# Attention units placed inside the query and output projections of a decoder step, with rotary halves in tiles of their own

## What is computed

```python
q = (_rms(x, ln) @ w_q).reshape(B, L, N_HEADS, HEAD_DIM)      # 16 heads of 64, 4 K/V heads
q = _rope(_rms(q, q_norm), pos)       # rotary: halves x1, x2 of 32 -> x1 cos - x2 sin, x2 cos + x1 sin
s = einsum('...qhgd,...khd->...hgqk', q, k) * HEAD_DIM ** -0.5  # window of 128 keys back
s = where(mask, s, NEG_INF); m = maximum(max(s), sink); p = exp(s - m)
o = einsum('...hgqk,...khd->...qhgd', p / (sum(p) + exp(sink - m)), v)
x = x + o.reshape(B, L, N_HEADS * HEAD_DIM) @ w_o
```

## Time and profile before

| | |
|---|---|
| median of 3 runs | 1662.77 us (1653.1 to 1663.02) |
| the profiled execution, its time | 1662.77 us |
| its span, first to last instruction | 1661.0 us |
| TensorE busy | 1611.2 us (97%), 11258 matmuls |
| DVE, ACT, POOL busy | 818.8, 492.5, 153.5 us |
| mean granted TensorE clock | 0.975 |

### The profile page before, as it was taken

The page is one execution under the profiler, slowest core; times in us unless marked ns, Lnnn a source line. Parts: engine busy times, 40 slices in busy tenths (PEclk is TensorE's granted clock), DMA queues, the critical chain, the costliest instruction groups (busy, mean ns, idle before and its releaser), DMA issues.

```text
span 1661.0 us, 26879 instructions
## 1 busy us (share of the span) xinstructions
PE 1611.2 (97%) x11258; PEld 1466.0 (88%) x11258; DVE 818.8 (49%) x1018; ACT 492.5 (30%) x745; POOL 153.5 (9%) x147
## 2 busy tenths in 40 slices
PE   7999999999999899999999999989999999999997
PEld 7679868968967899999999998865599999999997
DVE  6447337527535754334434575456755443433342
ACT  4233143133223322222212351135723221222221
POOL 0010000001001420000000131222331000000001
PEclk9999999999999999999999999975999999999999
DMA  6346226217224152222232222100023222232223
GB/s 231 106 165 214 83 96 225 86 58 262 81 74 155 52 179 76 92 86 93 84 102 76 89 89 77 54 6 1 1 77 97 81 89 89 81 97 89 89 76 105
DMA packets 49678, 164.40 MB, mean 99 GB/s; under 512 B 5664, under 2 KB 5728, under 8 KB 49568
## 3 DMA queue, kind: packets, MB, share of 16 engines
q1 hardware_dynamic: 41472, 134.23, 24.7%
q0 software_dynamic: 7408, 26.78, 4.4%
q10 hardware_dynamic: 720, 2.26, 0.3%
HBM read 141.82 MB, written 23.46 MB: 100 GB/s over the span
## 4 chain that ended last, share of the span: by engine, by line
PE 90%; DVE 5%; DMA 2%; ACT 1%; issue 1%; POOL 0%; ACTq 0%; DVEq 0%; POOLq 0%
PE ps L354 67%; PE ps L368 8%; PE ps L841 2%; PE ps L1123 2%; PE ps L835 2%; PE ps L1145 2%; DVE arena L1165 1%; DMA out_st_s<-arena 1%; PE ps L823 1%; PE ps L1134 1%; PE ps L855 1%; DMA arena<-in_state 1%; DVE xg_lo L1171 1%; PE ps L1037 1%; DMA w_raw<-in_w 1%
## 5 line engine op out<-in xcount | busy, mean ns | idle before, releaser
L354 PE MATMUL ps<-xg_hi,w_hi 128*128 128x272 f32 x1728 | 360.5, 290 | 15.3 <-DVE xg_lo L1171 8.3
L354 PE MATMUL ps<-xg_hi,w_lo 128*128 128x272 f32 x1728 | 358.0, 289 | 0.0
L354 PE MATMUL ps<-xg_lo,w_hi 128*128 128x272 f32 x1728 | 356.8, 288 | 0.0
L337 ACT ACTIVATE w_hi<-w_raw 128x1024 fp32r<-128x1024 f32 x220 | 227.2, 1052 | 368.6 <-PE ps L354 209.5
L342 DVE TENSOR_TENSOR w_lo<-w_raw,w_hi 128x1024 fp32r<-128x1024 f32 x220 | 281.6, 1297 | 63.5 <-ACT w_hi L337 57.9
L354 PE MATMUL ps<-pr_hi,w_hi 128*128 128x272 f32 x1440 | 304.5, 291 | 7.0 <-DVE pr_lo L1165 3.7
L354 PE MATMUL ps<-pr_hi,w_lo 128*128 128x272 f32 x1440 | 301.3, 289 | 0.0
L354 PE MATMUL ps<-pr_lo,w_hi 128*128 128x272 f32 x1440 | 300.4, 288 | 0.0
L354 PEld LDWEIGHTS ps<-xg_hi,w_hi 128*128 128x128 f32 x1728 | 273.0, 189 | 25.7 <-issue 12.7
L354 PEld LDWEIGHTS ps<-xg_lo,w_hi 128*128 128x128 f32 x1728 | 272.1, 189 | 0.0
L354 PEld LDWEIGHTS ps<-xg_hi,w_lo 128*128 128x128 f32 x1728 | 270.3, 189 | 0.0
(11 more groups left out here) (198 smaller groups left out, 1296.6 us busy)
## 6 DMA issues: line engine op xcount, KB each, us to landing
w_raw<-in_w SPq DMA_DIRECT2D x220, 512.0 KB, 3.4
arena<-in_state SPq DMA_DIRECT2D x32, 512.0 KB, 4.8
out_st_s<-arena POOLq DMA_DIRECT2D x32, 512.0 KB, 4.0
x<-in_x ACTq DMA_DIRECT2D x4, 544.0 KB, 6.2
out_y<-x POOLq DMA_DIRECT2D x8, 272.0 KB, 2.3
out_st_p<-arena SPq DMA_DIRECT2D x4, 512.0 KB, 2.8
arena<-in_dec POOLq DMA_DIRECT2D x4, 256.0 KB, 3.0
arena<-in_cache_v POOLq DMA_DIRECT2D x1, 1024.0 KB, 8.7
```

Source lines behind the costliest of these rows:

```text
L337: nc.scalar.activation(w_hi[:, n.c % 4, :], w_raw[:, n.c % 2, :], ACT.Copy).then_inc(w_hi_done, 1)
L354: last = pe.matmul(ps[:, 2 * bank_pair + s, 0:HT], w_of(w, k), xm[:, k, s * HT:(s + 1) * HT], start=(k == 0 and w == 0 and xi == 0), stop= ...
```

## The change

Queries, K and the K cache are laid out so that one tile holds the first rotary halves of all four K/V heads (32 rows each) and another the second halves. The rotation by matmul is gone: DVE does both products and the sum on tiles (`turned_by`), in place, with the gain. The squares of q go from ACT to POOL, K's norm is taken on one tile, and q is copied out of PSUM by ACT in halves of 272 columns.

A prompt unit is now a chunk and one query head of each of the four K/V heads. Its scores are matmuls of 32 rows in four row groups, accumulated over the two halves, into four banks; two units are issued at once. The values are eight matmuls of 128 columns that alternate between two groups of 64 output rows. The sample is one unit with all four K/V heads: products in 32 x 32 tiles, 264 scores a row for four pairs of sequences, values through a block-diagonal copy for the new tokens.

The query and output projections are cut into halves of columns, and the output projection also into two halves of its sum over k: 16 steps of 24 matmuls and 32 of 12. Tables SCORES, EXPS, TURNS and SUMS say at which step each part of each unit is issued, on all engines alike. The output partial sums are added to x step by step (`x_half`). POOL issues the cache writes ahead of the squares and divisions. The sample's cached V is loaded by ACT's queue at step 17. The output weights are reordered for it.

```diff
+LAST_BANKS = (6, 7, 4, 5)
+T_BANK, SUM_BANK = 6, 7
+QSUM_COL, SSUM_COL = 0, 16
+
+
+H_Q, H_A, H_B, H_C, H_D = 0, 16, 24, 32, 40
+SCORES = {5 + n: (n, n + 1) for n in range(0, 12, 2)} | {H_A + 4: (12,), H_A + 6: (13, 14), H_B + 2: (15, 16)}
+EXPS = {6 + n: n for n in range(12)} | {H_A + 5: 12, H_A + 7: 13, H_B + 1: 14, H_B + 3: 15, H_B + 5: 16}
+TURNS = {7 + n: n for n in range(10)} | {H_A + 2: 10, H_A + 4: 11, H_A + 7: 12, H_B + 1: 13, H_B + 3: 14, H_B + 5: 15, H_B + 7: 16}
+SUMS = (4, 8, 12, H_A + 1)
...
+            gp.wait_ge(va_done, 1)
             gp.dma_start(A["cv_p"], v_att[:, 4, :]).then_inc(caches_out, 16)
             for b in range(B):
                 gp.dma_start(A["cv_s"][b, WIN - TD:WIN, :], v_att[TD * b:TD * b + TD, 0, :]).then_inc(caches_out, 16)
             gp.wait_ge(kout_done, 2)
-            k_out = sqsum[:, 0:512].rearrange("p (a b) -> p a b", a=2)
...
+            def q_squares(i):
+                j, x_ = i // 2, i % 2
+                gp.wait_ge(q_raw, 2 * i + 2)
+                gp.wait_ge(q_sums, j)
+                gp.wait_ge(k_sums, 1)
+                nc.gpsimd.tensor_tensor(nrm[:, x_, :], q_of(j)[:, x_, :], q_of(j)[:, x_, :], ALU.mult).then_inc(q_sq, 1)
+
+            def probs(p):
+                n, (_, d, _) = unit_of(p), small_of(p)
+                den = small[:, d:d + 4]
+                gp.wait_ge(att_den, p + 1)
+                if n is None:
+                    nc.gpsimd.tensor_tensor(p_new, S_s[:, :, 256:264], den.unsqueeze(2).broadcast_to([P, 4, 8]), ALU.mult)
+                    nc.gpsimd.tensor_tensor(S_s[:, :, 0:256], S_s[:, :, 0:256], den.unsqueeze(2).broadcast_to([P, 4, 256]), ALU.mult).then_inc(att_p, 1)
+                else:
+                    S, w0 = S_of(n), first_key(n)
+                    nc.gpsimd.tensor_tensor(S[:, :, w0:256], S[:, :, w0:256], den.unsqueeze(2).broadcast_to([P, 4, 256 - w0]), ALU.mult)\
+                        .then_inc(att_p, 1)
+
+            for h in range(H_C):
+                if h in range(2, H_A + 1, 2):
+                    q_squares(h // 2 - 1)
+                if h in EXPS:
+                    probs(EXPS[h])
             gp.wait_ge(caches_out, 16 * (2 + 2 * B))
...
+            def raw_q(h):
+                i, s = h // 2, h % 2
+                half_ready(act, h)
+                if h == 12:
+                    act.wait_ge(att_s, 4)
+                nc.scalar.activation(q_of(i // 2)[:, i % 2, halves_of(s)], ps[:, h % 2, 0:HT], ACT.Copy).then_inc(q_raw, 1)
+
...
+            def probs_t(p):
+                n = unit_of(p)
+                act.wait_ge(att_tr, p + 1)
+                if n is None:
+                    nc.scalar.activation(pt_s.rearrange("p (a b) q -> p a (b q)", a=2), ps[:, T_BANK:T_BANK + 2, :], ACT.Copy).then_inc(att_pt, 1)
+                    return
                 if n >= 2:
-                    act.wait_ge(att_pv, NKV + n - 1)
-                nc.scalar.activation(ar(A_PPT[n % 2], 2, 512)[:, k0:2, :], ps[:, 4 + k0:6, :], ACT.Copy).then_inc(att_pt, 1)
-
-            def outs(n):
-                c, g = units[n]
-                u, lo_p = g // 2, 64 * (g % 2)
-                act.wait_ge(att_pv, NKV + n + 1)
-                nc.scalar.activation(xg_hi[lo_p:lo_p + 64, 4 * u:4 * u + 4, tok(c + 1)],
-                                     ps[lo_p:lo_p + 64, 6 + n % 2, :].rearrange("p (j t) -> p j t", j=4), ACT.Copy).then_inc(att_hi, 1)
-
-            for n in range(-DEPTH, len(units)):
-                if 0 <= n + 1 < len(units):
-                    probs_t(n + 1)
-                if n + DEPTH < len(units):
-                    exps(n + DEPTH)
-                if n >= 0:
-                    outs(n)
-            for m in range(KT):
-                split_hi(act, Index(N_ATT + 12 + 2 + m))
-                act.wait_ge(x_done, KT + m + 1)
-                gained_hi(m, G_FFN1, pr_hi, pg_hi_done)
+                    act.wait_ge(att_pv, pos_of(n - 2) + 1)
+                w0 = first_key(n)
+                src = ps[:, T_BANK:T_BANK + 2, :].rearrange("p b (g w) -> p (b g) w", g=2)
+                nc.scalar.activation(pt_of(n)[:, :, w0:256], src[:, :, w0:256], ACT.Copy).then_inc(att_pt, 1)
+
...
+            for h in range(H_D + KT + 1):
+                if h - 1 in TURNS:
+                    outs(TURNS[h - 1])
+                if 1 <= h <= H_A:
+                    raw_q(h - 1)
+                if h == 1:
+                    act.wait_ge(k_means, 1)
+                    nc.scalar.activation(k_root_t, k_root_t, ACT.Sqrt, bias=eps, scale=1.0 / HD).then_inc(k_root, 1)
+                if h < H_A and h % 2 == 0:
+                    split_hi(act, Index(N_ATT + 6 + h // 2))
+                if h == 4:
+                    act.wait_ge(kout_mm, 1)
+                    for a, n in ((0, P), (1, 32)):
+                        nc.scalar.activation(k_out[0:n, a, :], ps[0:n, 2 + a, 0:256], ACT.Copy).then_inc(kout_done, 1)
+                if h in (5, 9, 13):
+                    keep_q(h // 4 - 1)
+                    fac_root(h // 4 - 1, 1)
+                if h == H_A + 1:
+                    split_hi(act, Index(N_ATT + 14))
+                    split_hi(act, Index(N_ATT + 15))
+                    keep_q(3)
+                    act.dma_start(v_cache, A["cache_v"].rearrange("b w f -> w b f")).then_inc(vc_in, 16)
+                if h == H_A + 2:
+                    fac_root(3, 1)
+                    act.wait_ge(rs_means, 1)
+                    nc.scalar.activation(r_s, r_s, ACT.Sqrt, bias=eps, scale=1.0 / HD).then_inc(rs_root, 1)
+                if h in EXPS:
+                    exps(EXPS[h])
+                if h in TURNS:
+                    probs_t(TURNS[h])
+                if h in range(H_B + 2, H_C + 2, 2):
+                    split_hi(act, Index(N_ATT + 16 + (h - H_B - 2) // 2))
+                if h in (H_D + 2, H_D + 4):
+                    split_hi(act, Index(N_ATT + 20 + (h - H_D - 2) // 2))
+                if h > H_D:
+                    m = h - H_D - 1
+                    act.wait_ge(x_done, KT + m + 1)
+                    gained_hi(m, G_FFN1, pr_hi, pg_hi_done)
...
+            def square_sums(j):
+
+                pe.wait_ge(q_sq, 2 * j + 2)
+                pe.wait_ge(att_pt, len([h for h in TURNS if h <= SUMS[j]]))
...
+                for i in range(2):
+                    j, c, w0 = n // NCH, n % NCH + i, first_key(n + i)
+                    for x_ in range(2):
+                        for g in range(NKV):
+                            r = slice(32 * g, 32 * g + 32)
+                            last = pe.matmul(ps[:, 2 + g, 256 * i + w0:256 * i + 256], q_of(j)[r, x_, tok(c + 1)],
+                                             k_of[r, x_, NS_TOK + P * (c - 1) + w0:NS_TOK + P * (c + 1)], start=(x_ == 0), stop=(x_ == 1))
+                    last.then_inc(att_s, 1)
...
+            for h in range(H_A):
+                i, s = h // 2, h % 2
+                n = N_ATT + 4 + i
+                if h == 0:
+                    pe.wait_ge(k_raw, 2)
+                if s == 0:
+                    pe.wait_ge(w_lo_done, n + 1)
+                pe.wait_ge(q_raw, max(h - 1, 0))
+                part(h % 2, s, n % 4, 0, pr, 0, range(0, 2), KT)
+                if h == 3:
+                    pe.wait_ge(k_ready, 1)
+                    for a, t in ((0, tok(4)), (1, slice(0, NS_TOK))):
+                        for x_ in range(2):
+                            last = pe.transpose(ps[0:t.stop - t.start, 2 + a, x_ * P:x_ * P + P], k_of[:, x_, t], ident)
+                    last.then_inc(kout_mm, 1)
+                if h in SCORES:
+                    scores(SCORES[h])
+                part(h % 2, s, n % 4, 0, pr, 0, range(2, 4), KT)
+                turn_of(h)
+                last = part(h % 2, s, n % 4, 0, pr, 0, range(4, 8), KT)
+                last.then_inc(blocks if h in ENDS_BLOCK else half_mm, 1)
+                if h in TURNS:
+                    values(TURNS[h])
+                if h in SUMS:
+                    square_sums(SUMS.index(h))
+
...
+                part(bank, s, n % 4, (m % 2) * 512, xg, first, range(0, 1), 4)
+                if h in SCORES:
+                    scores(SCORES[h])
+                part(bank, s, n % 4, (m % 2) * 512, xg, first, range(1, 2), 4)
+                turn_of(h)
+                last = part(bank, s, n % 4, (m % 2) * 512, xg, first, range(2, 4), 4)
+                last.then_inc(blocks if h in ENDS_BLOCK else half_mm, 1)
+                if h in TURNS:
+                    values(TURNS[h])
+                if h in SUMS:
+                    square_sums(SUMS.index(h))
...
+            def turned_by(t, g, raw_ready, at, square_done, at_sq, x_):
+                dve.wait_ge(raw_ready, at)
+                stt(rt[:, x_, :], t[:, x_, :], g + x_, sin_a)
+                dve.wait_ge(square_done, at_sq)
+                stt(t[:, x_, :], t[:, x_, :], g + x_, cos_a).then_inc(v_chain, 1)
+                ch.k += 1
+                if x_ == 1:
```

(55 more changed lines are left out.)

705 lines of the change are left out of this document (308 added, 397 removed).

## The result

The changed kernel takes 1631.86 us (median of 4, 1630.72 to 1638.13) where the kernel before took 1661.85 beside it: 0.984 of it, 95% interval 0.982 to 0.987. The prediction was 1638. The medians lie 30.0 us apart where 25 were forecast. The profiled execution of the kernel after is the slowest of its four (1638.13 us; the others took 1630.72 to 1632.97). Its span is 1636.0 us against 1661.0, 25.0 us less, so that this one execution meets the sum to the tenth is chance. The total came out right; several of its terms did not.

What follows compares the result with a forecast made beforehand. TensorE was taken as the bound almost everywhere. The new stretch summed to 108.4 + 98.6 + 7.4 + 5 + 4 = 223.4 us against 248.4, a gain of 25 from 1662.8, giving 1638 us; range 1606 to 1670.

Steps and rivals of the forecast that it cites:

- The POOL stall: After step 4, TensorE waits 6.5 us for POOL's squares, queued behind cache writes that wait for ACT's K copy.
- The end stall: At the last FFN's first block, TensorE waits 7.4 us for gained tiles, delayed by DVE's remainders and splits.
- The other hand-offs: Steps 16 to 47: waits at eight transpose copies, steps 16 to 18 and the last three units, 13.2 us together.
- Scores: Prompt units: 16 records at 0.12 us, bounded by weight load, 1.9 us a unit; ends of range 1.0 and 4.0.
- The sample's products: Sample unit: 64 records of 256 columns in 32 x 32 tiles, 3.9 us, and 64 of 8 columns, 2.5 us.
- Even steps on the query side: Even steps among 7 to 15: ACT's chain takes 7.0 us against TensorE's 5.1, so ACT sets their length.
- query side: Steps 0 to 15, query projection with square sums, first scores and nine units: 108.4 us.
- Behind but not last: Steps 7 to 15: DVE's work of 6.1 us a step, of a mean of 8, does not hold up TensorE.
- DVE's queue: Rival: DVE's work plus waits for ACT's exponentials come last, 1.5 us in each of 17 steps: 1663 us, chance 0.13.
- The clock: After two stalls, TensorE does about 8 us of work at half clock, which costs 4 us.
- changes of tile shape: Units and sample: about three changes a unit and a few for the sample, 55 at 0.09 us, 5 us.
- full overlap: Rival: scores take 1.0 us a unit, cheaper sample, halved output hand-offs, no clock loss: 1610 us, chance 0.2.

Runs made afterwards that it cites:

- the run with the other order: Changed kernel with both halves of a head's score matmuls issued in a row before the next head: 1636.07 us, 0.986 of the kernel before.
- filling one wait: Changed kernel plus 44 discarded matmuls where TensorE waits for POOL's squares ahead of the first square sums: 1628.69 us, against 1635.23 beside it.
- the five edits: Changed kernel with late K cache writes, earlier first rotation, denominators before masks, gained halves for the last FFN and later weight splits: 1604.0 us, 0.966 of the kernel before.
- the run on one row group: Changed kernel with all heads' prompt score matmuls reading rows 0 to 31: 1691.14 us, 1.021 of the kernel before.

## Why the prediction was right, step by step

**The POOL stall** was forecast at 6.5 and was 5.9, at the place and for the queue named; taking the writes away removed it alone. **The end stall** was forecast at 7.4; it was 5.1 us of waits. The 7.4 itself does not follow from its terms: eight tiles at 2.3 us and two splits at 2.35 are 23.1, and even the rounded 24 is only 6.7 over 17.3. Half clock in the next 10 us comes on top: the FFN starts 34.0 us earlier than before (1219.37 against 1253.36), the span is 25.0 shorter, so 9 us were lost behind that point (7.4 forecast for the stall, and 2 of clock). **The other hand-offs** of steps 16 to 47 were forecast at 13.2 and the waits there sum to 17.2, but at other places: 8.9 of them at steps 16 and 18 (4.2 forecast), one of 2.8 in the last units (5.6 forecast), and 0.36 at only three of the eight copies.

**Scores: the term that was mis-sized.** Eight pairs at 3.8 us were priced at 30.4. At full clock a pair takes 2.01 us, or 1.59 where one unit is of chunk 0, 14.4 in all, 16 us less; with three of them at about half clock (2.6 to 2.9) the eight took 18.9. The choice between the earlier trace rows went to the wrong row: two-column matmuls at 0.12 us a record show what one full-height matmul after another costs, not what a record costs whose neighbour works on other rows., four times as fast, was the nearer kin, because there other columns worked meanwhile; that direct neighbours are apart is not needed, as the run with the other order shows (2.13). The Trainium skill ("TensorE: Matmul & The Clock Gate", Part 3, measured speedup) gives 3.07 times for four row tiles of 512 columns; the 3.6 times measured here at equal clock, with 128 and 256 columns in float32, decides. The sample's products were priced 6.4 and take 4.4 us (3.66 and 0.71), nearly all of it in the records of 8 columns.

**Even steps on the query side: wrong.** ACT's chain of 7.0 us against 5.1 of TensorE was to cost 1.9 at four steps, 7.6 us. No wait for ACT stands in the list between 1006 and 1115.6, for two reasons. At steps 8 and 12 the transposes came so late for DVE's sake that ACT had long finished its exponentials; at step 12 it was idle for 3.5 us before its copy. At steps 10 and 14 ACT did run without a gap from the result copy on, but the unit is of chunk 0 and its exponentials take 1.8 us, not the 2.9 that were priced for every step. At step 10 (ACT's copy):

```profile
1073.15 1.01 ACT L753 ACTIVATE arena<-ps 128x1024 f32<-128x1024 f32 x1
```

The transposes end at 1073.0 and the values start at 1074.4, 5.6 us after those of step 9 instead of 7.0. Whether ACT would come last with wide exponentials and no wait for DVE, no run shows.

**DVE: right in the mean, wrong in the order.** Its load was forecast at 6.1 of 8 us a step, 76%; from step 7 on (1043 to 1115.6) it is busy 54.6 of 72.6 us, 75%. "Behind but not last" failed all the same at steps 8, 12, 16 and 18, 15.4 us of waits, of which 4.2 were in the sum. The prediction divided the rotation evenly over the steps (a quarter each), but it stands in one piece of 3 us ahead of the remainder. And its price of 1.0 us an operation was too low where POOL works beside it. In the kernel after one takes 0.78 us while POOL does no arithmetic, and two take 3.09 beside POOL's division, as shown above; the low part of a tile for the last FFN, priced 1.0 too, takes 1.78 in the median of eight:

```profile
1017.10 0.78 DVE L1472 SCALAR_TENSOR_TENSOR arena<-arena,gain 128x544 f32<-128x544 f32 x1
```

The rival "DVE's queue" had the mechanism, with 1.5 us in each of 17 steps; it was 3 to 5 us in four.

**The clock: wrong by its size.** Two stalls were to cost 4 us. On the query side 108.4 forecast, less 12.0 for six pairs of scores, less 7.6 for ACT, less 0.6 at the POOL stall, plus 6.6 for DVE, plus half of the 5 us for changes of tile shape, makes 97.3; measured 109.5. The 12 us that are left I put down to the clock: 31 us at half clock there, 5 of them idle, cost half of 26. This is a remainder that fits and not a measurement of its own; what the runs show is the direction and the size (filling one wait gave 3 to 6.5 us, all of it clock).

So the total is right in large part by luck. The scores (16 us), ACT (7.6), the sample (2) and the two stalls (0.6 and 2.3) were given 28.5 us too much. Against them stand 6.6 us of waits at steps 8 and 12, 4.0 at the hand-offs of the second half, and, as what is left of 223.4, some 18 us of clock beyond the forecast's 4 (13 if the medians are taken in place of this execution). The rival "full overlap" (1610) was right about the scores. It would have been near in time too with DVE's order in hand: the kernel with the five edits takes 1604.

## What stays open

What exactly sets the clock back, and how much of the 66 us belongs to which wait, is not settled. Half clock follows each of the longer waits in the kernel after, but it also stood with TensorE busy without a gap: in the run on one row group, in the units of the kernel before, and in part behind the filled wait. That the kind of matmul plays a part is a rival that no run tests. Why the five edits together gain more than one by one is open too. That POOL lengthens DVE's instructions is shown by one form in two orders (3.09 and 1.47 us), not by a run made for it. Whether the remainder ahead of the masks would give the rest of the 12 us was not tried.

## What to carry to other kernels

Small matmuls that share no rows of the array, or no columns, cost little more than a quarter when there are four (3.6 times less on four row groups, four times on four column groups). Take the price from a row where several groups are at work, not from one where every matmul takes the whole height. When work is interleaved into a stream of products, write down for each hand-off what stands in front of it in the helper's queue at that step, since a mean load of 75% hides a burst of 3 us, and a burst beside POOL's work is twice as long. Where two waits end within 1 us, do not judge either edit by time alone: read what is left of the wait. Count such a wait of TensorE at more than its length (here 18 us of them were worth 28 by the medians), for the half clock behind it.
